# First four mixer outputs in four accumulator banks, statistics behind the third pack, value transposes one slot later, the fourth head's root behind the exponentials

## The chip, the core and the metric

The kernel runs on one core of a Trainium2 chip. A core has TensorE (PE, matrix products from SBUF into PSUM; PEld is its weight load), VectorE (DVE), ScalarE (ACT), GpSimd (POOL) and SyncE (SP), which here only issues the loads of the weights. The engines run their own instruction streams and meet only by semaphores. PSUM has eight banks of 128 x 512 fp32, called `ps[:, 0]` to `ps[:, 7]` here; bank 7 is `STAT`. The metric is the device time of one execution, in microseconds; lower is better.

## What is computed

Two transformer blocks on x of 512 tokens x 1024 features, all in fp32. The change touches only the first part of the first block, the hybrid mixer:

```python
def hybrid_mixer(h, w_in, lam_q1, ..., subln_g, w_out, rel_bias, layer_idx):
    proj = h @ w_in
    (aq, ak, av, bq, bk, bv, cq, ck, cv, iq, ik, iw) = jnp.split(
        proj, np.cumsum(IN_SPLITS)[:-1].tolist(), axis=-1)
    ...
    o_a = diff_attention(aq, ak, av, lam, lam_init, subln_g, rel_bias[:, :A_HEADS])
    o_b = dilated_attention(bq, bk, bv, rel_bias[:, A_HEADS:A_HEADS + B_HEADS])
    o_c = dsa_attention(cq, ck, cv, iq, ik, iw, rel_bias[:, A_HEADS + B_HEADS:])
    o = jnp.concatenate([o_a, o_b, o_c], axis=-1).astype(h.dtype)
    return o @ w_out

def first_block(x, mem, ...):
    h = rmsnorm(x, norm_mix[l])
    x = x + hybrid_mixer(h, ...)
    h = rmsnorm(x, norm_mem[l])
    x = x + memory_attention(h, rmsnorm(mem, norm_memkv[l]), ...)
    h = rmsnorm(x, norm_ffn[l])
    x = x + conv_ffn(h, ...)
```

`diff_attention` has four heads, each the difference of two softmaxes, and ends with an rmsnorm per head (`subln_g`). `dsa_attention` selects 128 keys per query by an indexer. The rest (memory attention, the convolutional feed-forward layer, and the second block with four feed-forward layers, a pool and long-convolution mixer and a latent attention) is outside the change.

## The kernel before

**Packs.** Every weight matrix is cut into packs of 128 outputs x 1024 inputs (512 KB). SP loads pack n into `raw[:, n % 2]`, ACT rounds it to `whi` (`split_high`), and a subtraction gives the rest, `wlo`; this is done by POOL (`split_low`, L693) for all packs but the first `FIRST` = 2, where DVE does it (`first_low`, L2000). SP loads pack n once pack n-2 is split. The input is split the same way, into `lin_hi` and `lin_lo`, 8 chunks of 128 x 512. A pack then takes 24 matmuls: for each chunk high x high (L741), high x low (L742), low x high (L743). So three passes give the precision of fp32.

**Start.** ACT and DVE make the eight chunks, and beside them the squares of x and their sum (`sumsq`). PE runs packs 0 and 1 chunk by chunk (L798 to L814), pack 1 two chunks behind pack 0, so that work starts before all of x is there. Before the last chunk of pack 1 it takes the column sum of `sumsq` (`stats(0)`, L755). ACT takes the root of it (L1360), DVE its reciprocal (L1904): `rstd`, by which every output of the mixer is scaled when DVE evicts it from PSUM (L2133). Then PE makes the bias rows (L818, L819), which DVE adds to a mask (L2027, L2028) before the reciprocal.

**Slots.** The 30 packs of the mixer run in slots n = 0 to 29, the outputs in order (`MIX_ORDER`): six indexer tiles, four heads of query, key and value of the differential attention, then the other heads. In slot n each engine does its pack work and then what `between(n)` asks: the indexer in slots 6 to 11, the scores of the differential attention from slot 10, `top_round`s of the key selection on DVE in slots 8 to 28, and so on. Pack n goes into bank n % 2, so its first matmul waits for the eviction of pack n-2. The engines' orders are written out by hand; the constants name the slots:

- Head h of the differential attention is multiplied out in slot 16 + 4h, its squares are summed by PE into bank 6 in slot 17 + 4h (`diff_sum`, L892), DVE reads the sum in slot 18 + 4h (L2119, into `diff_root[h]`), ACT takes the root in slot 19 + 4h (`diff_roots`, L1516: a logarithm and an exponential, with an activation table load before each), DVE scales the head in slot 20 + 4h (L2123).
- `turn_values(v, n)` (L841 to L851) transposes value tile v on PE into bank 6 too, in the slots `V_AT` = (12, 13, 15, 18, 22, 24, 27, 31); ACT copies it back (`store_values`). It must wait until DVE has read the sums made before.

**Pair steps.** After slot 29 come 18 steps s = 0 to 17 for the other eight heads, two at a time: PE scores (L939), DVE maximum (L2150), ACT exponentials (L1586), DVE division (`pair_norm`, L2160), PE transposes (`pair_turn`, L968), ACT copies (L1594), and every fourth step PE's product (L982). From s = 2 each step has one pack of the memory projection too (`memory_pack`, L954 to L956), whose one bank must be evicted (L2182) before the next. The step s also runs `between(30 + s)`. In step 3 ACT rounds all four heads of the differential attention to `o_hi` (L1610), in step 4 DVE makes their rests `o_lo` (L2172). Then `project_out` multiplies the eight chunks of `o_hi` and `o_lo` by `w_out`, each chunk of the first output waiting for the semaphore `mixed_low`.

## Time and profile before

| | us |
|---|---|
| median of 3 runs | 2858.08 |
| lowest, highest | 2857.74, 2867.32 |
| profiled execution, its time | 2862.86 |
| profiled execution, span of the trace | 2860.8 |
| PE busy | 2763.7 (97%) |
| PEld busy | 2180.9 (76%) |
| DVE busy | 1167.6 (41%) |
| POOL busy | 1123.0 (39%) |
| ACT busy | 1034.3 (36%) |
| mean DMA rate | 91 GB/s |

The views used are the page's chain of work that ended last, the timeline (one row for an instruction or a run of like instructions: start, duration of the whole run, engine, line, operation, tiles, count, and in brackets how long the engine had been idle and who released it), and tables of busy time by stretch. A matmul's duration overlaps with the next one's, so the distance of two starts is what it costs. PEclk is the clock granted to TensorE as a share of full speed: 1.00 is 2.4 GHz, 0.50 is 1.2 GHz.

### The profile page before, as it was taken

What the parts mean: (1) busy time and instruction counts of PE and PEld (TensorE: products, weight loads), DVE (VectorE), ACT (ScalarE), POOL (GpSimd) and SP (SyncE); (2) the same over time, 40 slices, a digit from 0 to 9 for tenths busy, and PEclk for the clock granted to TensorE, in tenths of its full rate; (3) what the DMA queues carried; (4) which work ended last, traced back from release to release, by engine and by line L of the source; (5) the groups of instructions that cost most, each with busy time, mean ns of one, the idle gap of its engine ahead of it and who ended that gap; (6) DMA issues with size and microseconds to landing.
All of it is one profiled execution on the core that took longest, in us unless ns stands there. A gap on an engine that the chain in (4) does not pass through costs nothing.

```text
span 2860.8 us, 35435 instructions
## 1 busy us (share of the span) xinstructions
PE 2763.7 (97%) x12322; PEld 2180.9 (76%) x12322; DVE 1167.6 (41%) x1919; ACT 1034.3 (36%) x1579; POOL 1123.0 (39%) x477
## 2 busy tenths in 40 slices
PE   7999999999999999999999999999999989999997
PEld 5766787888887888856878888888888744788886
DVE  4766534555535223138783222222221356322212
ACT  3445534444333232251223222233222557322222
POOL 2323442444454444522314444444444420444443
PEclk9999999999999999999999999999999999999998
DMA  4323331333332323321203333332333210233233
GB/s 148 113 82 103 111 96 45 97 95 96 100 107 87 97 94 97 116 81 64 73 23 103 95 95 97 109 103 90 101 95 108 84 52 1 81 95 98 93 103 103
DMA packets 77383, 259.70 MB, mean 91 GB/s; under 512 B 8871, under 2 KB 12455, under 8 KB 77048
## 3 DMA queue, kind: packets, MB, share of 16 engines
q1 hardware_dynamic: 68976, 242.77, 27.4%
q10 hardware_dynamic: 8328, 15.88, 1.7%
q8 instruction: 49, 0.80, 0.1%
q14 instruction: 30, 0.25, 0.0%
HBM read 252.59 MB, written 6.03 MB: 90 GB/s over the span
## 4 chain that ended last, share of the span: by engine, by line
PE 91%; DVE 5%; issue 2%; ACT 2%; DMA 0%; ACTq 0%; SPq 0%; DVEq 0%
PE ps L741 26%; PE ps L742 26%; PE ps L743 26%; PE ps L1274 1%; PE ps L1288 1%; PE ps L1302 1%; PE ps L1280 1%; PE ps L1089 1%; PE ps L1021 0%; PE ps L1031 0%; PE ps L954 0%; PE ps L1137 0%; PE ps L955 0%; PE ps L956 0%; PE ps L939 0%
## 5 line engine op out<-in xcount | busy, mean ns | idle before, releaser
L695 POOL TENSOR_TENSOR wlo<-raw,whi 128x1024 fp32r<-128x1024 f32 x453 | 1109.0, 2451 | 1699.1 <-ACT whi L1335 1698.3
L741 PE MATMUL ps<-lin_hi,whi 128*128 128x512 f32 x2208 | 871.4, 395 | 15.7 <-DVE waves_tmp L2296 6.6
L742 PE MATMUL ps<-lin_lo,whi 128*128 128x512 f32 x2208 | 863.5, 391 | 0.0
L743 PE MATMUL ps<-lin_hi,wlo 128*128 128x512 f32 x2208 | 863.2, 391 | 0.0
L1335 ACT ACTIVATE whi<-raw 128x1024 fp32r<-128x1024 f32 x455 | 476.7, 1053 | 524.1 <-PE ps L743 476.0
L741 PEld LDWEIGHTS ps<-lin_hi,whi 128*128 128x128 f32 x2208 | 417.3, 189 | 110.2 <-issue 15.3
L742 PEld LDWEIGHTS ps<-lin_lo,whi 128*128 128x128 f32 x2208 | 417.3, 189 | 88.2 <-issue 2.6
L743 PEld LDWEIGHTS ps<-lin_hi,wlo 128*128 128x128 f32 x2208 | 417.0, 189 | 88.0
L741 PE MATMUL ps<-act_hi,whi 128*128 128x512 f32 x880 | 342.6, 389 | 0.0
L743 PE MATMUL ps<-act_hi,wlo 128*128 128x512 f32 x880 | 342.4, 389 | 0.0
L742 PE MATMUL ps<-act_lo,whi 128*128 128x512 f32 x880 | 342.3, 389 | 0.0
L1917 DVE SCALAR_TENSOR_TENSOR x<-ps,x 128x512 f32 x72 | 49.8, 692 | 486.2 <-PE ps L743 486.2
L1950 DVE TENSOR_TENSOR up<-ps,rstd 128x512 f32<-128x512 f32 x88 | 60.8, 691 | 393.9 <-PE ps L743 393.9
L1426 ACT ACTIVATE act_hi<-hidden 128x512 f32 (+1 forms) x88 | 55.6, 632 | 458.8 <-DVE hidden L1973 458.8
L741 PEld LDWEIGHTS ps<-act_hi,whi 128*128 128x128 f32 x880 | 165.2, 188 | 35.4 <-POOL wlo L695 0.8
L743 PEld LDWEIGHTS ps<-act_hi,wlo 128*128 128x128 f32 x880 | 165.2, 188 | 34.6
L742 PEld LDWEIGHTS ps<-act_lo,whi 128*128 128x128 f32 x880 | 165.2, 188 | 34.5
L1350 ACT ACTIVATE scratch<-x 128x512 f32 x72 | 45.6, 634 | 262.0 <-DVE x L1917 262.0
L1950 DVE TENSOR_TENSOR gate<-ps,rstd 128x512 f32<-128x512 f32 x88 | 60.9, 692 | 188.2 <-PE ps L743 187.3
L741 PE MATMUL ps<-o_hi,whi 128*128 128x512 f32 x256 | 100.5, 392 | 1.7 <-DVE o_lo L2478 1.7
L742 PE MATMUL ps<-o_lo,whi 128*128 128x512 f32 x256 | 99.6, 389 | 0.0
L743 PE MATMUL ps<-o_hi,wlo 128*128 128x512 f32 x256 | 99.6, 389 | 0.0
(351 smaller groups left out, 2648.6 us busy)
## 6 DMA issues: line engine op xcount, KB each, us to landing
raw<-in_packs SPq DMA_DIRECT2D x459, 512.0 KB, 3.5
table<-bias_scratch ACTq DMA_DIRECT2D x12, 256.0 KB, 2.9
bias_scratch<-biasrow ACTq DMA_DIRECT2D x16, 160.0 KB
x<-in_x_t SPq DMA_DIRECT2D x4, 512.0 KB, 7.8
out_t<-x ACTq DMA_DIRECT2D x8, 256.0 KB, 2.2
bias_scratch<-biasrow ACTq DMA_DIRECT2D x4, 320.0 KB
mem<-in_mem_t ACTq DMA_DIRECT2D x1, 1024.0 KB, 7.7
pool_count<-in_pool_count ACTq DMA_DIRECT2D x1, 1024.0 KB, 4.8
```

Source lines behind the costliest of these rows:

```text
L695: pool.tensor_tensor(wlo[:, n % 4, :], raw[:, n % 2, :], whi[:, n % 4, :].bitcast(F32), ALU.subtract).then_inc(low_split, 1)
L741: pe.matmul(target, wh, hi[:, k, :], start=(k == 0), stop=False)
L742: pe.matmul(target, wh, lo[:, k, :], start=False, stop=False)
L743: mm = pe.matmul(target, wl, hi[:, k, :], start=False, stop=(k == total - 1))
L1089: pe.matmul(ps[:, 4 + c // 2, :], ones[:, :], filt_sq[t % 2][:, c * T:(c + 1) * T], start=(t == 0 and c % 2 == 0), stop=(t == QT - 1 and c ...
L1274: mm = pe.matmul(ps[:, 2 * p + h, :], q_nope[r:r + 64, 2 * g + p, cut], k_nope[r:r + 64, 2 * g + p, :], start=True, stop=False)
L1280: mm = pe.matmul(ps[:, j, :], q_rope[r:r + 32, g, cut], k_rope[r:r + 32, :], start=False, stop=True)
L1335: act.activation(whi[:, n % 4, :], raw[:, n % 2, :], ACT.Copy).then_inc(high_split, 1)
L1350: act.activation(squares[:, d % 2, :], x[:, row, :].rearrange("p a t -> p (a t)"), ACT.Square).then_inc(squares_ready, 1)
L1426: act.activation(act_hi[:, bass.ds(f, 1), :].rearrange("p a t -> p (a t)"), h_buf, ACT.Copy).then_inc(hidden_high, 1)
L1917: dve.scalar_tensor_tensor(out=xc, in0=ps[:, j, :], scalar=factor, in1=xc, op0=ALU.mult, op1=ALU.add).then_inc(outs_done, 1)
L1950: dve.tensor_tensor(target, ps[:, 2 * g + side, :], rstd[:, :], ALU.mult).then_inc(outs_done, 1)
```

## The change

It has three parts.

**Start.** Packs 0 to 3 get banks 0 to 3 (`mixer_bank`), so packs 2 and 3 wait for no eviction, packs 4 and 5 for those of packs 0 and 1. Pack 1 runs three chunks behind pack 0 (`LAG`). `stats(0)` and the bias rows come behind pack 2. DVE splits pack 2 as well (`FIRST_LOW` = 3); POOL begins with pack 3 and waits until the squares are summed. SP loads pack 1 before the third and fourth quarter of x. ACT does the chunks first and most squares afterwards; DVE sums all squares behind the chunks. The root on ACT is one slot later, and the bias addition on DVE moves from before the reciprocal to slot 1.

**Value transposes.** `V_AT` becomes (12, 13, 15, 19, 23, 24, 28, 32): tiles 3, 4, 6 and 7 one slot later.

**Fourth head.** Its root leaves step 1 for the end of step 16, behind the last exponentials and copies; its scale, rounding and rest are in step 17, and its buffer is `scratch[:, 0]`. Heads 0 to 2 are rounded in steps 0 to 2 (one each) and their rests made in steps 1 to 3, where before all four stood together in steps 3 and 4. The first output of `project_out` takes its chunks in the order 0, 1, 2, 4, 5, 6, 3, 7.

```diff
-FIRST = 2
+FIRST, FIRST_LOW = 2, 3
+LAG = 3
+def mixer_bank(n):
+    return n if n < 4 else n % 2
+MIXED_ORDER = (0, 1, 2, 4, 5, 6, 3, 7)
+LAST_HEAD = HEADS - 1
-V_AT = (12, 13, 15, 18, 22, 24, 27, STEPS_AT + 1)
+V_AT = (12, 13, 15, 19, 23, 24, 28, STEPS_AT + 2)
...
         load_x(0)
         load(0, None)
-        for q in range(1, 4):
+        load_x(1)
+        load(1, None)
+        for q in range(2, 4):
             load_x(q)
...
-        pool.wait_ge(low_split, FIRST)
-        for n in range(FIRST, 4):
+        pool.wait_ge(low_split, FIRST_LOW)
+        pool.wait_ge(squares_summed, DC)
+        for n in range(FIRST_LOW, 4):
             split_low(n, None)
...
         for n in range(FIRST, N_MIXER):
-            pe.wait_ge(outs_done, n - 1)
-            pack("mixer", None, 4, n, ps[:, n % 2, :], LIN)
+            if n >= 4:
+                pe.wait_ge(outs_done, n - 3 if n < 6 else n - 1)
+            pack("mixer", None, 4, n, ps[:, mixer_bank(n), :], LIN)
+            if n == 2:
+                pe.wait_ge(dve_order, 1)
+                stats(0)
+                bias_rows()
+                pe.wait_ge(ident_arrived, 16)
             between(n)
...
         for n in range(N_MIXER):
             split_high(AHEAD + n)
-            if n == 0:
+            if n == 1:
                 root(0)
...
-            if s == 3:
-                act.wait_ge(diff_scaled, HEADS)
-                for h in range(HEADS):
-                    act.activation(o_hi[:, h, :], diff_out[:, h, :], ACT.Copy).then_inc(out_high, 1)
             if s >= 5 and s % 4 == 1:
+                if s == LAST_STEP - 1:
+                    diff_high(LAST_HEAD)
...
+            if s < LAST_HEAD:
+                diff_high(s)
+            if s == PAIR_STEPS:
+                diff_roots(LAST_HEAD)
...
-            if s == 4:
-                for h in range(HEADS):
-                    dve.wait_ge(out_high, h + 1)
-                    dve.tensor_tensor(o_lo[:, h, :], diff_out[:, h, :], o_hi[:, h, :].bitcast(F32), ALU.subtract).then_inc(mixed_low, 1)
+            if s == LAST_STEP - 1:
+                diff_scale(LAST_HEAD)
+                diff_low(LAST_HEAD, 7)
...
+            if 1 <= s <= LAST_HEAD:
+                diff_low(s - 1, s)
```

Here `diff_high(h)` waits for the scaled head h and writes `o_hi[:, h]`, `diff_scale(h)` waits for its root and scales it, `diff_low(h, n)` waits for `out_high` = n and writes `o_lo[:, h]`.

**Where it moves instructions.** DVE at the start, from the first split of a pack to the first eviction; L2002 and L2031 are the split of a pack, L2010 and L2037 a chunk, L2018 and L2048 a sum of squares. Before:

```order
7 L2002 TENSOR_TENSOR wlo<-raw,whi 128x1024 [waits high_split,dve_order]
8 L2010 SCALAR_TENSOR_TENSOR lin_lo<-x,cols,lin_hi 128x512 [waits chunk_high,x_quarter0_arrived]
9 L2010 SCALAR_TENSOR_TENSOR lin_lo<-x,cols,lin_hi 128x512 [waits chunk_high]
10 L2018 TENSOR_TENSOR sumsq<-sumsq,scratch 128x512 [waits squares_ready]
11 L2010 SCALAR_TENSOR_TENSOR lin_lo<-x,cols,lin_hi 128x512 [waits chunk_high,x_quarter1_arrived]
12 L2018 TENSOR_TENSOR sumsq<-sumsq,scratch 128x512 [waits squares_summed,squares_ready]
13 L2010 SCALAR_TENSOR_TENSOR lin_lo<-x,cols,lin_hi 128x512 [waits chunk_high]
14 L2002 TENSOR_TENSOR wlo<-raw,whi 128x1024 [waits high_split]
```

After:

```order
7 L2037 SCALAR_TENSOR_TENSOR lin_lo<-x,cols,lin_hi 128x512 [waits chunk_high,x_quarter0_arrived,dve_order]
8 L2031 TENSOR_TENSOR wlo<-raw,whi 128x1024 [waits high_split]
9 L2037 SCALAR_TENSOR_TENSOR lin_lo<-x,cols,lin_hi 128x512 [waits chunk_high]
10 L2037 SCALAR_TENSOR_TENSOR lin_lo<-x,cols,lin_hi 128x512 [waits chunk_high,x_quarter1_arrived]
11 L2031 TENSOR_TENSOR wlo<-raw,whi 128x1024 [waits high_split]
...
17 L2031 TENSOR_TENSOR wlo<-raw,whi 128x1024 [waits high_split]
18 L2048 TENSOR_TENSOR sumsq<-sumsq,scratch 128x512 [waits squares_ready]
19 L2048 TENSOR_TENSOR sumsq<-sumsq,scratch 128x512 [waits squares_summed,squares_ready] x7
```

The sums no longer stand between the chunks; all eight follow the third split.

PE in slots 17 to 19, the packs' own matmuls left out; L862 and L876 are scores, L873 and L887 transposes of probabilities, L892 and L906 the sum of squares of head 0, L850 and L864 the transpose of value tile 3. Before:

```order
502 L892 MATMUL ps<-scratch,ones 128x512 [waits v_stored,diff_squares]
...
531 L873 MATMUL ps<-ident,probs 128x128 [waits mixer_copied,mixer_ready]
532 L873 MATMUL ps<-ident,probs 128x128 x2
533 L850 MATMUL ps<-ident,proj 128x128 [waits diff_sums_read,v_stored,outs_done]
534 L850 MATMUL ps<-ident,proj 128x128 x3
...
561 L873 MATMUL ps<-ident,probs 128x128 [waits mixer_copied,mixer_ready]
```

After:

```order
502 L906 MATMUL ps<-scratch,ones 128x512 [waits v_stored,diff_squares]
...
531 L887 MATMUL ps<-ident,probs 128x128 [waits mixer_copied,mixer_ready]
532 L887 MATMUL ps<-ident,probs 128x128 x2
...
559 L887 MATMUL ps<-ident,probs 128x128 [waits mixer_copied,mixer_ready]
560 L887 MATMUL ps<-ident,probs 128x128 x3
561 L864 MATMUL ps<-ident,proj 128x128 [waits diff_sums_read,v_stored,outs_done]
```

The value transpose stands one whole pack and its scores later; what it waits for stays the same.

ACT in steps 0 to 3; L1586 and L1609 are the exponentials, L1594 and L1617 the copies of transposed probabilities, L1518 and L1519 the fourth head's root, L1523 and L1546 the copy of a value tile. Before:

```order
164 L1586 ACTIVATE pair_probs,small<-pair_probs,small 128x256 x2
165 L1335 ACTIVATE whi<-raw 128x1024
166 L1518 ACT_TABLE_LOAD
167 L1518 ACTIVATE diff_late<-diff_late 128x512
168 L1519 ACT_TABLE_LOAD
169 L1519 ACTIVATE diff_late<-diff_late 128x512
170 L1523 ACTIVATE proj<-ps 128x512
171 L1594 ACTIVATE pair_probs_t<-ps 128x128 x2
172 L1586 ACTIVATE pair_probs,small<-pair_probs,small 128x384 x2
...
178 L1610 ACTIVATE o_hi<-proj 128x512 x4
```

After:

```order
158 L1622 ACTIVATE o_hi<-proj 128x512
159 L1609 ACTIVATE pair_probs,small<-pair_probs,small 128x256 x2
160 L1355 ACTIVATE whi<-raw 128x1024
161 L1617 ACTIVATE pair_probs_t<-ps 128x128 x2
162 L1622 ACTIVATE o_hi<-proj 128x512
163 L1609 ACTIVATE pair_probs,small<-pair_probs,small 128x384 x2
164 L1355 ACTIVATE whi<-raw 128x1024
165 L1546 ACTIVATE proj<-ps 128x512
...
167 L1622 ACTIVATE o_hi<-proj 128x512
```

The two table loads and two activations of the root are gone from between the exponentials; the roundings stand singly.

## Rows read from the trace of the kernel before

**Rows 1.** The page's chain of work that ended last, shares by engine.
```profile
PE 91%; DVE 5%; issue 2%; ACT 2%; DMA 0%; ACTq 0%; SPq 0%; DVEq 0%
```

**Rows 2.** Timeline of PE at the start: start, duration, line, count, idle before.
```profile
10.75 0.76 PE L808 MATMUL ps<-lin_hi,whi 128*128 128x512 f32 x1 [10.75 <-DVE lin_lo L2010]
...
17.22 0.51 PE L808 MATMUL ps<-lin_hi,whi 128*128 128x512 f32 x1 [2.29 <-DVE wlo L2002]
...
28.11 1.10 PE L755 MATMUL ps<-sumsq,ones 128*128 128x512 f32 x2 [0.79 <-DVE relb_apart L2019]
...
30.76 0.38 PE L819 MATMUL ps<-onehot,relb_apart 32*96 32x128 f32 x2
...
36.93 0.76 PE L741 MATMUL ps<-lin_hi,whi 128*128 128x512 f32 x1 [5.79 <-issue]
...
45.04 0.39 PE L741 MATMUL ps<-lin_hi,whi 128*128 128x512 f32 x1
...
50.48 0.39 PE L741 MATMUL ps<-lin_hi,whi 128*128 128x512 f32 x1
```

**Rows 3.** Timeline of the other engines at the start.
```profile
8.72 1.23 DVE L2002 TENSOR_TENSOR wlo<-raw,whi 128x1024 fp32r<-128x1024 f32 x1 [2.65 <-ACT whi L1335]
...
21.39 5.23 POOL L695 TENSOR_TENSOR wlo<-raw,whi 128x1024 fp32r<-128x1024 f32 x2 [20.94 <-ACT whi L1335]
...
24.29 3.67 DVE L2018 TENSOR_TENSOR sumsq<-sumsq,scratch 128x512 f32<-128x512 f32 x2
...
29.24 0.69 ACT L1360 ACTIVATE rstd<-ps,small 128x512 f32<-128x512 f32 x1 [5.75 <-PE ps L755]
...
32.11 3.34 DVE L1904 RECIPROCAL rstd<-rstd 128x512 f32<-128x512 f32 x1
...
36.14 1.29 DVE L2133 TENSOR_TENSOR proj<-ps,rstd 128x512 f32<-128x512 f32 x2
```

**Rows 4.** Busy time by stretch: length, PE, PEld, DVE, ACT, POOL, then PEclk, DMA.
```profile
10.70:28.60 17.90, 14.77 (x46) 10.95 (x47) 15.55 (x22) 10.70 (x16) 5.23 (x2) 0.90 0.43 141
36.90:50.40 13.50, 13.47 (x48) 10.93 (x49) 1.22 (x2) 2.55 (x3) 2.40 (x1) 0.80 0.27 82
162.60:171.50 8.90, 8.80 (x28) 6.94 (x28) 3.73 (x10) 7.60 (x12) 2.38 (x1) 0.66 0.24 78
198.90:206.50 7.60, 7.58 (x28) 5.95 (x28) 2.67 (x6) 6.14 (x10) 2.39 (x1) 0.78 0.12 27
260.80:267.00 6.20, 6.20 (x33) 4.37 (x34) 2.67 (x9) 4.37 (x12) 2.37 (x1) 0.72 0.27 73
120.00:140.00 20.00, 20.00 (x99) 16.01 (x98) 19.34 (x51) 12.38 (x30) 7.18 (x3) 1.00 0.37 114
```

**Rows 5.** Timeline of PE in slots 18 and 22: the value transposes.
```profile
162.69 1.08 PE L850 MATMUL ps<-ident,proj 128*128 128x128 f32 x4 [2.51 <-DVE diff_early L2119]
...
198.92 0.66 PE L850 MATMUL ps<-ident,proj 128*128 128x128 f32 x4 [3.14 <-DVE diff_early L2119]
```

**Rows 6.** Timeline of the pair steps, several engines.
```profile
255.62 1.28 ACT L1518 ACT_TABLE_LOAD   x1
...
259.52 0.75 DVE L2123 SCALAR_TENSOR_TENSOR proj<-proj,small,diff_late 128x512 f32<-128x512 f32 x1 [3.19 <-ACT diff_late L1519]
...
260.80 1.12 PE L968 MATMUL ps<-ident,pair_probs 128*128 128x128 f32 x4 [2.59 <-DVE pair_probs L2160]
...
270.47 4.63 DVE L2172 TENSOR_TENSOR o_lo<-proj,o_hi 128x512 fp32r<-128x512 f32 x4
...
272.04 2.52 POOL L695 TENSOR_TENSOR wlo<-raw,whi 128x1024 fp32r<-128x1024 f32 x1 [2.17 <-ACT whi L1335]
...
275.58 0.36 PE L954 MATMUL ps<-mem_hi,whi 128*128 128x256 f32 x1 [2.77 <-DVE mem_k L2182]
...
337.06 1.08 ACT L1594 ACTIVATE pair_probs_t<-ps 128x512 f32<-128x512 f32 x2 [1.43 <-PE ps L968]
...
342.57 0.50 PE L741 MATMUL ps<-o_hi,whi 128*128 128x512 f32 x1
```

124 lines of the change are left out of this document (67 added, 57 removed).

## The prediction

> **What bounds the kernel now.** I read the chain of work that ended last first: TensorE holds 91% of it [rows 1], so only what lets PE start earlier, closes an idle stretch of PE or raises its clock can move the time. Then the waits of PE over the mixer, from the start to 345 us, and behind each the timeline, to see who was late. They are few. Work starts at 10.75 us, then PE waits 2.29, 0.79 and 5.79 us [rows 2]; 2.51 and 3.14 us in slots 18 and 22 [rows 5]; 2.59 and 2.77 us in the pair steps [rows 6]. A wait costs more than its length: the table by stretch shows what PE was granted after it. After the 5.79 us it ran at 0.80 for 13.5 us, after 2.51 at 0.66 for 8.9 us, after 3.14 at 0.78 for 7.6 us, after 2.59 at 0.72 for 6.2 us, while the undisturbed stretch from 120 to 140 has 1.00 [rows 4]. The lost time is (1 - PEclk) x length: 2.7, 3.0, 1.7 and 1.7 us. After the 2.77 us I see no such fall, so a wait may cost its length alone. The levels are 1.2 and 2.4 GHz.
>
> **Start, removed.** Before, pack 4 starts at 50.48 [rows 2]. For the changed kernel I lay out PE's work anew. A pack at full clock is the distance of packs 3 and 4, 50.48 - 45.04 = 5.44 us [rows 2].
> - First matmul: the first split of a pack by DVE ended at 8.72 + 1.23 = 9.95 [rows 3], and PE then waited for the second thing, a chunk, until 10.75. Now that chunk is made ahead of the split: 10.0.
> - Packs 0 to 2 without a break: 3 x 5.44 = 16.3 us.
> - Low clock at the beginning: 0.10 x 17.9 = 1.8 us were lost in the first stretch, 2.7 us in pack 2 [rows 4]. I take 2.5, between them and nearer the upper one, since this stretch too follows a long rest.
> - Statistics and bias rows: 28.11 to 30.76 + 0.38 = 31.14, less the three matmuls (0.7) between them: 2.3 us [rows 2].
> - Pack 3: 5.4 us.
>
> Sum: 10.0 + 16.3 + 2.5 + 2.3 + 5.4 = 36.5 for the start of pack 4, **14.0 us earlier**.
>
> It holds only if nobody is late. *Chunks:* pack 1 follows three chunks behind, so its split is wanted when PE has done three chunks, at 10.0 + 3 x 1.28 (low clock) = 13.8. Before, it came at about 17.2 [rows 2], because ACT waited for pack 1's load, the last of six; now it is the fourth, some 3 us earlier, and DVE should be done at 13.3. *DVE's split of pack 2:* after the last chunk (about 16.7), so about 18.6; wanted near 23.4. *Sums:* eight of about 0.8 us behind it, to about 25.3; wanted at 28.8. Before, two sums took 3.67 us and stood beside two splits of POOL, 21.39 to 26.6 [rows 3]; now POOL waits for them, and I take them unhindered. *POOL:* its two splits took 5.23 us [rows 3], so 2.6 each: pack 3 is split at about 28, wanted at 31.1; pack 4 at about 30.5, wanted at 36.5. *Evictions:* here the change adds the waits for the evictions of packs 0 and 1 ahead of packs 4 and 5. Statistics start at 28.8; root 1.13 later (29.24 - 28.11), 0.69 long; reciprocal 3.34; from its end to the first eviction 0.69, the eviction about 0.65 [rows 3]: 35.4. PE wants the bank at 36.5. This is the nearest margin, 1.1 us, and since both sides hang on the same statistics, it doesn't move with the clock much. The bias addition (two operations of the first's kind, 1 us) now stands behind the second eviction, not ahead of the reciprocal. Queued behind it are ACT's copies of the bias rows to DRAM and ACT's next split, wanted only by pack 6 at 47. SP's queue gets one load ahead of two others, which costs the late quarters of x under 3 us; they are wanted from about 13.
>
> **Value transposes.** In slot 18 PE waits until DVE has read the sum of squares, which DVE does near the end of its slot, behind an eviction that itself waits for pack 18. One slot later the read is 6 us old. The wait goes with the clock's fall: slot 18 gives 2.51 + 3.0 = 5.5 us, slot 22 gives 3.14 + 1.7 = 4.8 us [rows 4, 5]; the transposes themselves (0.66 us at mostly full clock [rows 5]) only move. What is late next? In slots 19 and 23 ACT has the root, four operations of about 3.9 us, ahead of the copy that PE's next transposes need; it can start once the sum is read and ends about 3 us before the copy could start anyway. **10.3 us**, bounds 8 and 10.5.
>
> **Pair steps.** The root in step 1 ran on ACT from 255.62 and DVE's scale came to wait 3.19 us for it, until 259.52; `pair_norm` stood behind the scale, and PE waited 2.59 us [rows 6]. With the root gone DVE can do the division about 2 us earlier. I count 1.8 of the 2.59 us, plus the clock's 1.7 us [rows 4]. The transposes of the last value tile leave step 1, where PE waits for the first division anyway, and stand in step 2, where nobody waits: 0.66 us lost [rows 5]. The 2.77 us wait was for an eviction that stood behind four rests of 4.63 us in all [rows 6]; they are spread over three steps now, and each follows the eviction. I count 2.5. Sum: 1.8 + 1.7 - 0.7 + 2.5 = 5.3; I take **5.0**, bounds 2 and 6.5.
>
> At this place a rule of the chip speaks against the change. The row: the four rests, two-input operations from SBUF, took 4.63 us where an eviction from PSUM of the same size takes 0.65 (1.29 for two [rows 3]), and a split of POOL ran from 272.04 to 274.56 among them [rows 6]; the last one ended just behind it. So a rest that meets a split can cost its length plus up to 2.5 us. The Trainium skill (SBUF — State Buffer, "SBUF: two separate sides") states why: a VectorE instruction with two SBUF inputs and a GpSimd instruction exclude one another for the whole instruction, and whoever starts first keeps the ports; so the trace agrees. By the rule four rests in a row meet one split and pay once, three rests in three steps can pay three times.
>
> **Fourth head at the end.** Its root now starts behind the last copies, 337.06 + 1.08 = 338.1, and ends at about 342.0; scale, rounding and rest follow by 344.3, the last chunk's rest by 345.4. PE starts the output projection at 342.57 [rows 6] and takes 0.68 us a chunk; with the fourth head seventh and the last product eighth it wants them at 346.7 and 347.3. Cost 0; without the new order it would wait some 2 us at the fourth chunk. ACT's splits of two later packs come 2 us later; they are wanted 5 us and more later.
>
> **Sum.** 14.0 + 10.3 + 5.0 + 0 = 29.3 us. The profiled execution took 2862.86 us, which gives 2833.6; it lies 4.8 above the median of the runs, and from the median 2858.08 I get **2828.8**. Nothing after the mixer changes, and PE bounds it there.
>
> **Rivals.**
> - *The sums stay slow.* At 3.67 / 2 = 1.84 us each [rows 3] they end at 18.6 + 14.7 = 33.3, POOL's split of pack 3 at 35.9, and pack 3 starts 4.8 us late, with 2.7 us of clock behind it. Start part 6.5, time 2836. For it: the rows' own price; against: POOL was at work then. Chance 0.10.
> - *The rests meet the splits.* Each of three rests is held up to 2.5 us and the next scores with it; if two reach PE, 5 us are lost and the first fall of the clock stays, 1.7. Pair part -2, time 2836. For it the row above; against, DVE had 2 to 3 us to spare in most steps. Chance 0.12.
> - *The change doesn't do what it says* in slots 19 and 23: ACT's root, copy and value copy in one slot are late for PE's next transposes, and the wait comes back one slot on. 2 to 3 of the 10.3 us remain, time 2836. Chance 0.06.
> - *Slower than before.* DVE, not PE, bounds the slots. DVE is busy 19.34 of 20 us from 120 to 140 [rows 4], and the two waits I remove are also its time to catch up. If the new phase of POOL's splits holds up a DVE operation in each slot by 2.4 us, PE waits for it and loses about as much again by the clock: 4.8 us a slot. From six slots on that eats the whole gain; in fourteen (12 to 25) it is 67 us, time 2896. Against it: PE is busy 20.00 in that same stretch, and DVE idles 5 us in slots 18 and 22 after the reads. Chance 0.03.
>
> **How the numbers follow.** Forecast 0.69. Its own range is 2826 to 2836 (start 12 to 15, slots 8 to 10.5, pair steps 2 to 6.5). The first three rivals lie at 2836, two of them together near 2843; so 2822 to 2842 holds 8 in 10, with the scatter of the runs (2857.74 to 2867.32). Half a percent, about what a measurement of this kernel can tell from no change, is 14.3 us: below 2843.8. That takes the start alone. Faster 0.90, within 0.5% 0.07 (two or three rivals at once), slower 0.03.
>
> **What would show it.** Pack 4's first matmul near 36.5, no wait of PE over 1 us between 14 and 160; no wait at the value transposes and PEclk 1.00 through slots 18 to 24; in the pair steps no wait over 1.5 us for DVE in steps 2 and 5; no wait for `o_lo` at the output projection. Wrong would be: a wait for POOL's `wlo` ahead of pack 3, for DVE's evictions ahead of pack 4, for chunks between 13 and 17, or rests of over 2 us in steps 1 to 3 with PE waiting behind them.

## The result and the profile after

The changed kernel takes **2833.12 us** (median of 4 runs, 2833.00 to 2835.70) against 2859.18 for the kernel before, measured beside it (4 runs, 2857.74 to 2867.32). The ratio is 0.9904, with a 95% interval of 0.9891 to 0.9916: about 27 us faster. The forecast was 2828.8 with a range of 2822 to 2842.

| | before | after |
|---|---|---|
| median, us | 2859.18 | 2833.12 |
| profiled execution: time, us | 2862.86 | 2835.70 |
| its span, us | 2860.8 | 2833.5 |
| waits of PE up to 345 us, without that for its first matmul | 24.3 | 5.0 |

First the waits of PE from the start to 345 us, after: engine, tile and line, what it waited for; us in total, times, longest.

```profile
PE ps L823 <- DVE wlo L2031: 10.2, 1, 10.2
PE ps L988 <- DVE pair_probs L2198: 4.6, 4, 2.0
PE ps L876 <- DVE small L2108: 0.4, 1, 0.4
```

Before there were nine such lines. The two of the start (2.29 and 5.79 us), both value transposes and the wait for `mem_k` in step 5 are gone; what is left, 4.6 us, waits for the division of the pair steps. Now the timeline of PE at the start, after. The rows answer to [rows 2]: the columns are start, duration, line, what it does, its count, and in brackets the idle time before it.

```profile
10.23 0.77 PE L823 MATMUL ps<-lin_hi,whi 128*128 128x512 f32 x1 [10.23 <-DVE wlo L2031]
...
28.83 1.02 PE L770 MATMUL ps<-sumsq,ones 128*128 128x512 f32 x2
...
30.72 0.38 PE L834 MATMUL ps<-onehot,relb_apart 32*96 32x128 f32 x2
31.02 0.50 PE L756 MATMUL ps<-lin_hi,whi 128*128 128x512 f32 x1
...
36.59 0.39 PE L756 MATMUL ps<-lin_hi,whi 128*128 128x512 f32 x1
```

Pack 4 starts at 36.59 instead of 50.48, and no bracket stands between 10.23 and 36.59. The first matmuls run at low clock all the same: until 14.64 they start 0.43 us apart, from 14.96 on 0.23. The column PEclk doesn't show this; two stretches, eleven matmuls in the first and 24 in the second:

```profile
10.23:14.90 4.67, 4.67 (x11) 3.72 (x12) 4.32 (x7) 4.57 (x8) 0.00 (x0) 1.00 0.99 358
15.00:20.00 5.00, 5.00 (x24) 4.10 (x23) 4.26 (x6) 3.47 (x6) 0.00 (x0) 1.00 0.32 98
```

The other engines there, answering to [rows 3]:

```profile
8.86 1.23 DVE L2031 TENSOR_TENSOR wlo<-raw,whi 128x1024 fp32r<-128x1024 f32 x1
...
16.83 1.23 DVE L2031 TENSOR_TENSOR wlo<-raw,whi 128x1024 fp32r<-128x1024 f32 x1 [0.53 <-ACT whi L1355]
17.97 6.26 DVE L2048 TENSOR_TENSOR sumsq<-sumsq,scratch 128x512 f32<-128x512 f32 x8
...
30.61 3.35 DVE L1933 RECIPROCAL rstd<-rstd 128x512 f32<-128x512 f32 x1 [5.81 <-ACT rstd L1380]
34.66 1.29 DVE L2171 TENSOR_TENSOR proj<-ps,rstd 128x512 f32<-128x512 f32 x2
```

```profile
24.37 5.03 POOL L709 TENSOR_TENSOR wlo<-raw,whi 128x1024 fp32r<-128x1024 f32 x2 [23.92 <-DVE sumsq L2048]
```

Eight sums take 6.26 us: each is 0.68 to 0.70 long, and they start 0.8 apart. Before, two took 3.67 beside POOL [rows 3], one of them 2.88. POOL starts when the sums are done. The busy time by stretch answers to [rows 4], in its columns; the first two stretches are the start and pack 4's, the next two follow the places of the old waits in slots 18 and 22, the last two begin with the first matmul after the two longest waits that are left:

```profile
10.70:28.60 17.90, 17.90 (x71) 14.54 (x71) 12.46 (x23) 12.34 (x17) 4.23 (x2) 1.00 0.41 138
36.60:50.10 13.50, 13.50 (x61) 11.20 (x60) 3.92 (x8) 4.56 (x5) 4.99 (x3) 1.00 0.46 155
148.70:157.60 8.90, 8.90 (x45) 7.02 (x44) 8.18 (x25) 8.78 (x12) 2.38 (x1) 1.00 0.25 79
179.50:187.10 7.60, 7.60 (x40) 5.95 (x39) 7.29 (x21) 7.54 (x14) 2.38 (x1) 1.00 0.30 78
229.40:239.40 10.00, 9.99 (x60) 7.81 (x61) 8.18 (x18) 8.34 (x21) 7.76 (x3) 0.83 0.34 106
287.10:297.10 10.00, 9.99 (x59) 7.09 (x60) 3.40 (x12) 3.68 (x9) 2.37 (x1) 0.83 0.32 97
```

In the third and fourth stretch PE is busy without a gap and PEclk is 1.00, where [rows 4] have 0.66 and 0.78. The pair steps, answering to [rows 6]:

```profile
229.41 0.53 PE L988 MATMUL ps<-ident,pair_probs 128*128 128x128 f32 x2 [1.97 <-DVE pair_probs L2198]
...
229.87 2.45 DVE L2130 TENSOR_TENSOR o_lo<-proj,o_hi 128x512 fp32r<-128x512 f32 x1 [0.32 <-ACT o_hi L1622]
...
287.11 0.66 PE L988 MATMUL ps<-ident,pair_probs 128*128 128x128 f32 x4 [1.74 <-DVE pair_probs L2198]
...
314.45 0.50 PE L756 MATMUL ps<-o_hi,whi 128*128 128x512 f32 x1
```

**Where the 27 us come from.** The same instruction is looked for in both timelines, and the differences of its starts are the gain so far:

| PE's instruction | before | after | gain so far | of this part |
|---|---|---|---|---|
| first matmul | 10.75 | 10.23 | 0.52 | 0.52 |
| pack 4 | 50.48 | 36.59 | 13.89 | 13.37 |
| scores of slot 20 | 178.24 | 158.83 | 19.41 | 5.5 |
| first pair scores | 250.86 | 226.51 | 24.35 | 4.9 |
| product of step 5 | 278.62 | 248.99 | 29.63 | 5.3 |
| output projection | 342.57 | 314.45 | 28.12 | -1.5 |
| end of the span | 2860.8 | 2833.5 | 27.3 | -0.8 |

Each of the two columns of starts is one profile. The last two rows give something back: the experiments show why for the first of them; the second lies within what profiles differ by behind the mixer (below).

### The profile page after: what moved, and what is told of

The parts are those of the page before. It is cut to its first block, busy times and chain, and to the rows that moved or that the text cites. A ratio compares the mean times of both kernels' runs of the same rounds, so it can differ in the third digit from the quotient of the medians.

```text
span 2833.5 us, 35433 instructions
## 1 busy us (share of the span) xinstructions
PE 2753.8 (97%) x12322; PEld 2176.3 (77%) x12322; DVE 1172.4 (41%) x1920; ACT 1034.5 (37%) x1579; POOL 1121.2 (40%) x476
## 4 chain that ended last, share of the span: by engine, by line
PE 92%; DVE 5%; ACT 1%; issue 1%; DMA 0%; ACTq 0%; DVEq 0%
PE ps L756 26%; PE ps L758 26%; PE ps L757 26%; PE ps L1294 1%; PE ps L1308 1%; PE ps L1322 1%; PE ps L1300 1%; PE ps L1109 1%; PE ps L974 1%; PE ps L1041 0%; PE ps L1051 0%; PE ps L975 0%; PE ps L976 0%; PE ps L959 0%; PE ps L876 0%
## 5 line engine op out<-in xcount | busy, mean ns | idle before, releaser
L756 PEld LDWEIGHTS ps<-act_hi,whi 128*128 128x128 f32 x880 | 165.2, 188 | 35.9 <-POOL wlo L709 0.8
```

What stands on the lines that cost most here:

```text
L756: pe.matmul(target, wh, hi[:, k, :], start=(chunk0 + at == 0), stop=False)
```

## Experiments

In each run the time is compared with the kernel before on the same chip. For differences of one or two us the starts of PE's instructions say more than the times, and this is why: from the output projection to the end all kernels run the same instructions, yet the profiles need 2513.5 to 2519.2 us for them.

**The parts alone.** Three kernels are the kernel before with one part of the change each.

*Start alone*, the kernel before with all of the change's first part; its core:

```diff
-FIRST = 2
+FIRST, FIRST_LOW = 2, 3
+LAG = 3
...
+def mixer_bank(n):
+    return n if n < 4 else n % 2
...
-        for q in range(1, 4):
+        load_x(1)
+        load(1, None)
+        for q in range(2, 4):
```

> The kernel before with the start part alone (four banks, statistics behind pack 2, loads, splits and squares in the new order). My theory, that the parts add up because PE alone bounds the mixer: pack 4 starts at 36.6 and everything behind it comes 13.9 us earlier, the waits at the value transposes (2.51 and 3.14 us) and in the pair steps stay as they were. Time 13.9 us under the kernel before, ratio 0.9951. Rival, that another engine takes part of it back (DVE bound in slots 10 to 28): pack 4 at 36.6, but the scores of slot 18 less than 13 us earlier, total gain under 10 us.

*Values alone*, the kernel before with

```diff
-V_AT = (12, 13, 15, 18, 22, 24, 27, STEPS_AT + 1)
+V_AT = (12, 13, 15, 19, 23, 24, 28, STEPS_AT + 2)
```

> The kernel before with the value transposes alone moved one slot. My theory, a wait costs its length plus a fall of the clock: no wait of PE in slots 18 and 22, PEclk 1.00 through slots 18 to 24, gain 5.5 + 4.9 = 10.4 us by the first scores of the pair steps, of which the last transpose (now in step 2) gives back up to 0.7. Ratio 0.9965. Rival, that only the waits count and the clock's fall comes from elsewhere: PEclk still falls in these slots and the gain is 5.7 us, ratio 0.998. Rival, ACT's root is late in slots 19 and 23: a new wait of PE for the copies there, gain under 5 us.

*Fourth head alone*, the kernel before with the third part of the change:

```diff
+MIXED_ORDER = (0, 1, 2, 4, 5, 6, 3, 7)
+LAST_HEAD = HEADS - 1
...
+            if s < LAST_HEAD:
+                diff_high(s)
+            if s == PAIR_STEPS:
+                diff_roots(LAST_HEAD)
```

> The kernel before with the fourth head's part alone: its root behind the exponentials, roundings and rests of heads 0 to 2 one a step, chunk order of the output projection. The last value tile is still turned in step 1. My theory: the waits of 2.59 us (step 2) and 2.77 us (step 5) and the clock's fall behind the first go, 2.59 + 1.7 + 2.77 = up to 7 us by the product of step 5; since PE's transposes of the value tile fill part of the wait of step 1, there is no fall of the clock there. Ratio 0.9976 to 0.998. Rival, the three rests each meet a split of POOL and reach PE: gain 0 to 3 us by step 5.

| | median, us | ratio to before (95%) | output projection at | earlier by |
|---|---|---|---|---|
| before | 2861.61 | | 342.57 | |
| start alone | 2849.95 | 0.9957 (0.9943 to 0.9971) | 329.62 | 12.95 |
| values alone | 2850.85 | 0.9963 (0.9949 to 0.9978) | 332.53 | 10.04 |
| fourth head alone | 2853.95 | 0.9975 (0.9964 to 0.9987) | 335.73 | 6.84 |
| all | 2833.12 | 0.9904 (0.9891 to 0.9916) | 314.45 | 28.12 |

The parts add up: 12.95 + 10.04 + 6.84 = 29.8 us of starts against 28.1 for all, and 0.43 + 0.37 + 0.25 = 1.05% of time against 0.96%, with each interval some 0.13% to either side. All three are needed for the result, the start and the values most. In start alone both waits at the value transposes stay (2.51 and 3.14 us); in values alone PE has no wait over 0.4 us between 100 and 242 us; in fourth head alone the waits of 2.59 and 2.77 us are gone. A part of the fourth head's 6.84 isn't its own: the first turn of the pair steps already stood at 251.47 instead of 253.76, 2.29 us earlier, ahead of anything that it changes there. Without it the parts make 27.5. Values alone loses again what it had ahead: its first turn of the pair steps stands 11.4 us earlier than before (242.38), but its wait of 2.95 us in step 5 is followed by the largest fall of all, 0.69 over 10 us, where the kernel before had none behind 2.77 us.

**The clock after a wait.** This kernel is the one before, with 13 matmuls of no use in slot 22, where PE waited 3.14 us; they write to a bank that nobody reads at that time.

```diff
+            if n == 22:
+                pe.wait_ge(mem_sums_read, 1)
+                for k in range(13):
+                    pe.matmul(ps[:, STAT, :], lin_hi[:, k % 8, 0:P], lin_hi[:, k % 8, :], start=True, stop=True)
```

> The kernel before with 13 extra matmuls of 512 columns in slot 22, ahead of the value transpose, into a bank that nobody uses then and that nobody reads: they add work that the result doesn't need and lie in the wait of 3.14 us. My theory, that the clock falls because PE stood idle: the wait shrinks to some 0.2 us, PEclk stays 1.00 behind it and pack 23 takes 5.4 instead of 7.2 us, so that the scores of slot 23 come 1.7 us earlier though PE does more. Slot 18 is as before. Total gain 1.7 us, ratio 0.9994, which the times can hardly tell; the trace decides. Rival, that the fall has another cause (time, power, the slots' load): PEclk about 0.78 from 199 to 206.5 as before, total no change or up to 1 us slower.

Measured: 2859.08 us (2856.59 to 2862.58), ratio 0.9992 (0.9982 to 1.0002), no difference that the times can show; the output projection stands at 340.67, 1.90 us earlier. The timeline of PE, and the two stretches of 10 us behind slot 22's and slot 18's transposes:

```profile
192.73 3.22 PE L917 MATMUL ps<-lin_hi 128*128 128x512 f32 x13
196.10 0.63 PE L850 MATMUL ps<-ident,proj 128*128 128x128 f32 x4 [0.16 <-DVE diff_early L2123]
```

```profile
196.10:206.10 10.00, 10.00 (x49) 7.92 (x50) 6.30 (x19) 8.26 (x16) 2.40 (x1) 1.00 0.22 57
162.70:172.70 10.00, 10.00 (x49) 7.92 (x50) 7.30 (x23) 9.22 (x14) 2.40 (x1) 1.00 0.20 70
```

Behind the filled wait PEclk is 1.00, as a cause in the idle time would have it (the kernel before has 0.83 there). But the second row spoils it as a proof: slot 18's wait of 2.52 us, untouched, has no fall behind it either, where the kernel before had the largest:

```profile
162.70:172.70 10.00, 10.00 (x37) 7.74 (x38) 4.59 (x14) 8.78 (x13) 2.38 (x1) 0.70 0.21 69
```

So the price of a wait is not fixed, and the filler alone doesn't show that idle time is the cause. All profiles of this study together, 14 with those of the two kernels, have 36 waits of 1.7 to 3.2 us between 100 and 345 us; I took PEclk over the 10 us behind each, as in the rows above, and (1 - PEclk) x 10 as lost:

| wait | how many | with a fall | lost by one, mean | most |
|---|---|---|---|---|
| 2.2 to 3.2 us | 16 | 12 | 1.5 us | 3.1 |
| 1.7 to 2.0 us | 20 | 10 | 0.8 us | 1.7 |
| 0.94 to 0.98 us, with no longer one in the next 10 us | 6 | 0 | 0 | 0 |

The wait of 1.73 us in step 13 is the cleanest case, since it is there in twelve of these profiles at the same place of the program, with the same work behind it: five have 0.83 behind it and seven 1.00. What decides between them these runs don't settle; it isn't the length of the wait.

The (1 - PEclk) x 10 is also not what a fall costs in time. Between two fixed instructions the distances are alike to 0.2 us but for the falls:

| profile | first pair scores to product of step 5 | product of step 5 to output projection |
|---|---|---|
| changed kernel, two profiles | 22.48, 22.47 (fall in step 1) | 65.46, 65.42 (fall in step 13) |
| POOL early (below) | 22.33 (fall) | 63.95 (none) |
| bias addition first (below) | 21.75 (none) | 63.95 (none) |

The fall in step 13, 1.7 by the clock, costs 1.5 us; the one in step 1, 1.7 as well, only 0.6 to 0.7. Without it PE comes earlier to step 2 and waits there 0.56 us for a division.

At the start there is a second sign that chance has a part. In nine profiles with the new start (the changed kernel twice, start alone, and six of the kernels below) the first matmul stands at 9.98 to 10.23, but the first one faster than 0.63 us comes between 13.3 and 15.8, and the statistics stand at 28.17 to 29.38. The Trainium skill (TensorE: Matmul & The Clock Gate, "What's actually happening") says that the window in which the chip looks at the engine runs free and doesn't start with the kernel, so that the moment of a switch depends on where in it the work lands. The spread at the start agrees with that; no run here shows the window itself, and none shows that it decides about the falls behind the waits.

**The last two waits.** Four kernels on one chip: the changed kernel once more, two edits to it, and both edits together.

The changed kernel again, as the yardstick:

> The changed kernel itself, once more, as the yardstick for the three kernels beside it. In its first profile 1.97 us of waiting in pair step 1 and 1.74 us in step 13 were each followed by a stretch of low clock (1.6 and 1.7 us lost), while the same waits had no fall behind them in some of the other profiles. Theory A (the fall belongs to the wait and to the place): a new profile of the same kernel shows both falls again, the product of step 5 starts at 249.0 and the output projection at 314.5 within 0.2. Theory B (whether a wait of 2 us is followed by a fall changes between executions): the times of the runs spread over 2 to 4 us, in steps, and the profile may show one fall, both or none, with the output projection at up to 3.3 us earlier than 314.45. Time by both: about 0.990 of the kernel before.

Its profile shows both falls again, 0.83 behind each wait, the product of step 5 at 248.94 and the output projection at 314.36, as its theory A says of a profile. The five runs lie in two groups, 2832.6 and 2832.8 and 2834.9 to 2835.6, as its theory B says of the times; only one of the upper group has a profile. So two profiles of the same kernel agree, and whether the lower group had fewer falls stays open.

The last value tile goes back to step 1, ahead of the turn of the pair probabilities:

```diff
-V_AT = (12, 13, 15, 19, 23, 24, 28, STEPS_AT + 2)
+V_AT = (12, 13, 15, 19, 23, 24, 28, STEPS_AT + 1)
```

> The changed kernel with the last turn of values put back into pair step 1, where it stood before, ahead of the turn of the pair probabilities. In the changed kernel TensorE waits there 1.97 us for the division, and before it waited 0.98 and 0.36 with the turn between. Theory A: the turn moves into the wait, 0.63 us of the following slot are saved, and the low clock after 1.97 us (0.84 in 232 to 236 in the first profile, 1.6 us lost in all) is gone too, since no wait is over 1 us: 0.6 to 2.3 us faster than the changed kernel. Theory B (the clock falls whatever the length): 0.6 us faster, no more. If the turn came from elsewhere late (its eviction is then the wait of 0.98), nothing is gained.

ACT rounds the weights behind its two copies in steps 4, 8 and 12, so POOL's split of them comes later:

```diff
-            if s < PAIR_STEPS + KV_FROM:
+            if s < PAIR_STEPS + KV_FROM and s not in (4, 8, 12):
                 split_high(N_MIXER + AHEAD + s)
...
                 pair_copy(2 * s - 2)
                 pair_copy(2 * s - 1)
+            if s in (4, 8, 12):
+                split_high(N_MIXER + AHEAD + s)
```

> The changed kernel with ScalarE's rounding of the weights in pair steps 4, 8 and 12 put behind the two copies of the transposed probabilities, so that GpSimd's split of those weights begins some 2 us later and does not stand beside VectorE's two divisions of 512 elements. Those took 4.41 us beside a split of GpSimd (4.92 us for two) where a pair of 384 took 0.75. Theory A (the wait of 1.74 us in step 13 comes from the lock of the two engines): the divisions fall to about 1 us, the wait of 1.74 is gone, with the low clock behind it where there was one; 1.7 to 3.4 us faster than the changed kernel. Theory B (the divisions are late for another reason, the roots and sums ahead of them): the wait stays at 1.7, no difference. If GpSimd's split then meets another operation of VectorE, or the weights come late for their pack, a new wait of 1 to 2.5 us stands in steps 5, 9 and 13, and it is slower.

Both:

> The two edits together: last turn of values in step 1, ScalarE's rounding behind the copies in steps 4, 8 and 12. If both work and are independent, the sum: 2.3 to 5.7 us faster than the changed kernel, no wait of TensorE over 1 us left in the mixer. If the length alone counts: 2.3 us. If the lock is not the cause of step 13's wait: 0.6 to 2.3 us.

| | median of runs, us (range) | ratio to before (95%) | PE's output projection at |
|---|---|---|---|
| changed kernel | 2834.90 (2832.62 to 2835.56) | 0.9906 (0.9892 to 0.9919) | 314.36 |
| last turn back | 2833.43 (2833.06 to 2834.51) | 0.9905 (0.9890 to 0.9920) | 312.75 |
| rounding late | 2832.46 (2827.83 to 2833.23) | 0.9899 (0.9885 to 0.9912) | 311.97 |
| both | 2829.75 (2827.62 to 2832.07) | 0.9889 (0.9874 to 0.9904) | 311.83 |

Last turn back, PE in step 1 and 2, and the stretch behind step 13's wait:

```profile
228.97 0.63 PE L864 MATMUL ps<-ident,proj 128*128 128x128 f32 x4 [0.98 <-DVE scratch L2160]
229.96 0.53 PE L988 MATMUL ps<-ident,pair_probs 128*128 128x128 f32 x2 [0.36 <-DVE pair_probs L2198]
235.35 0.70 PE L988 MATMUL ps<-ident,pair_probs 128*128 128x128 f32 x4 [0.95 <-DVE pair_probs L2198]
```

```profile
286.90:296.90 10.00, 9.99 (x72) 7.40 (x73) 4.84 (x16) 4.40 (x11) 2.35 (x1) 1.00 0.31 107
```

The wait of 1.97 is 0.98 + 0.36 again, and neither has a fall behind it. But step 2 now waits 0.95 where the changed kernel didn't. The product of step 5 comes 21.75 us behind the first pair scores, against 22.47 in the changed kernel with its fall and 21.75 in the profile of the table above that had none. So the edit gains nothing where the clock doesn't fall, and 0.7 us where it does. (By plain starts this is hidden: 248.81 against 248.94, since this profile was 0.58 late by the statistics already.) The other 1.5 us at the output projection come from step 13, whose wait of 1.73 this time had no fall behind it; that is not the edit's doing.

Rounding late does remove a wait. DVE in step 12 of the changed kernel and of the kernel with both edits, with POOL at the same time:

```profile
282.64 4.41 DVE L2198 TENSOR_SCALAR pair_probs<-pair_probs,small 128x512 f32<-128x512 f32 x2
...
281.85 4.92 POOL L709 TENSOR_TENSOR wlo<-raw,whi 128x1024 fp32r<-128x1024 f32 x2 [2.89 <-ACT whi L1355]
```

```profile
282.91 2.29 DVE L2200 TENSOR_SCALAR pair_probs<-pair_probs,small 128x512 f32<-128x512 f32 x2
...
288.65 3.99 DVE L2200 TENSOR_SCALAR pair_probs<-pair_probs,small 128x128 f32<-128x128 f32 x2
```

```profile
282.12 2.40 POOL L709 TENSOR_TENSOR wlo<-raw,whi 128x1024 fp32r<-128x1024 f32 x1 [2.89 <-ACT whi L1355]
...
287.79 4.77 POOL L709 TENSOR_TENSOR wlo<-raw,whi 128x1024 fp32r<-128x1024 f32 x2 [3.27 <-ACT whi L1355]
```

With one split of POOL beside them instead of two, the divisions of 512 take 2.29 instead of 4.41 us, and PE's wait of 1.74 is gone. The second split now meets the divisions of 128 that follow: 3.99 us instead of 0.48. They are early enough that PE waits only 0.36 for the second of them:

```profile
292.69 0.33 PE L988 MATMUL ps<-ident,pair_probs 128*128 128x128 f32 x1 [0.36 <-DVE pair_probs L2200]
```

So the cause is shown (a division of DVE stands still while POOL splits), and the edit moves the meeting to a place with more room. But its worth is small. Such a wait is new behind the products of step 5, 9 and 13 each (0.30, 0.36 and 0.37 us in rounding late), and from the product of step 5 to the output projection this kernel needs 63.69 us, against 63.95 with the old wait and no fall and 65.42 with the fall: 0.25 us gained where no fall comes, and 1.5 more where the clock would have fallen.

Both edits together have the lowest median of this study, 5.1 us below the changed kernel's, and no run of one lies among the runs of the other, though only 0.55 us lie between. The mixer accounts for half of it: the output projection stands 2.5 us earlier (0.1 at the first pair scores, 0.7 by the product of step 5, 1.7 behind it). Where the rest comes from isn't shown.

**Single steps of the start and of the rests.** Four more kernels on another chip, each the changed one with one thing taken back. The changed kernel itself didn't run beside them, so their times are set against the kernel before and against each other.

The loads in their old order:

```diff
         load_x(0)
         load(0, None)
-        load_x(1)
-        load(1, None)
-        for q in range(2, 4):
+        for q in range(1, 4):
             load_x(q)
+        load(1, None)
```

> The changed kernel with the second pack's weights loaded behind all four quarters of x again, as before the change; all else as changed. In the changed kernel TensorE begins at 10.2 and never waits in its first packs. Theory A (the order of the loads is what removed the wait of 2.29 us): it is back, 2 to 3 us, between 14 and 17 us, with more low clock behind it, and the third pack of the mixer, 31.02 in the changed kernel, starts 2 to 4.5 us later. Theory B (the chunks come sooner by the order of VectorE's and ScalarE's instructions, whatever the loads): no wait over 1 us, the third pack within 0.5 of 31.02. Time by A: 0.9915 of the kernel before instead of 0.9905, by B the same.

Measured: 2836.92 us (2833.73 to 2839.83), ratio 0.9921 (0.9898 to 0.9944).

```profile
16.63 0.80 PE L822 MATMUL ps<-lin_hi,whi 128*128 128x512 f32 x1 [2.42 <-DVE lin_lo L2036]
17.22 0.63 PE L823 MATMUL ps<-lin_lo,whi 128*128 128x512 f32 x1
```

The old wait is back, 2.42 us, in front of the fourth chunk, and pack 3 starts at 35.66 instead of 31.02. That is 4.6 us, a little above what I had given: nearly as much again as the wait is lost to low clock, since a matmul behind it takes 0.63 us until 21.1, where in the changed kernel it takes 0.39 from 14.96 on. This exchange of two loads alone is a third of the start's gain. At the output projection (316.86) only 2.4 of the 4.6 us are left: neither the wait of step 1 nor that of step 13 has a fall behind it in this profile, which by the table above is worth 0.7 and 1.5.

The bias addition ahead of the reciprocal:

```diff
+        dve.wait_ge(bias_ready, 1)
+        order(dve.tensor_tensor(biasrow[:, 0:512], ps[0:12 * APART, 4, :], maskrow[:, 0:512], ALU.add))
...
         norm(0)
...
-            if n == 1:
-                dve.wait_ge(bias_ready, 1)
```

> The changed kernel with the addition of the bias rows back ahead of the reciprocal on VectorE. It takes 0.67 and about 0.3 us, waits for the bias matmuls that end near 31.1, and pushes the reciprocal from 30.6 to about 32 and the two first evictions from 34.66 and 35.3 to about 36.0 and 36.7. Pack 4 started at 36.59 in the changed kernel with no wait. Theory A (the evictions hold pack 4, as the prediction's nearest margin of 1.1 us says): pack 4 waits 0.3 to 0.5, pack 5 not, less than 1 us in all. Theory B (the bank is not what it would wait for): no wait. Time by both within 0.1% of the changed kernel; what tells is the start of pack 4 and of the reciprocal.

```profile
31.52 3.34 DVE L1933 RECIPROCAL rstd<-rstd 128x512 f32<-128x512 f32 x1
...
35.55 2.48 DVE L2169 TENSOR_TENSOR proj<-ps,rstd 128x512 f32<-128x512 f32 x4
```

```profile
35.37 0.39 PE L756 MATMUL ps<-lin_hi,whi 128*128 128x512 f32 x1
...
36.29 0.50 PE L756 MATMUL ps<-lin_hi,whi 128*128 128x512 f32 x1
```

Pack 4 follows 0.92 us behind the last chunk of pack 3 instead of 0.67 (36.59 - 35.92 in the changed kernel): it waits 0.25 us for the first eviction, which ends near 36.2. So the margin ahead of pack 4 was there, and moving the bias addition away was worth a quarter of a microsecond. The time, 2830.97 us (ratio 0.9901, 0.9878 to 0.9925), can't show that: two runs lie at 2827.6 and 2827.9 and two at 2834.1 and 2834.2, though all four execute the same instructions. In its profile, taken from the first pair, the waits of 1.98 and 1.72 us in the pair steps stand as always and neither has a fall behind it.

Roundings and rests of three heads in one block each:

```diff
+            if s == 3:
+                for h in range(LAST_HEAD):
+                    diff_high(h)
...
+            if s == 4:
+                for h in range(LAST_HEAD):
+                    diff_low(h, h + 1)
...
-            if 1 <= s <= LAST_HEAD:
-                diff_low(s - 1, s)
```

> The changed kernel with the mixer's heads 0 to 2 rounded together in pair step 3 and their rests together in step 4, as before the change, in place of one head a step. Theory A (the block of rests on VectorE held the product of step 5, and GpSimd beside it made it longer: 4.63 us for four before, 2.45 for one beside GpSimd and 0.68 for one alone): three rests take 2 to 3.7 us, and TensorE waits 1 to 2.8 us in front of the products of step 5, which started at 245.9 in the changed kernel, 248.99 for the product that waited before. Some 1 to 3 us slower by step 5, partly given back since the rest that met GpSimd's splits in step 1 (1.97 us of waiting there for the division) is gone: that wait should then stay, because it follows the square root and the division ahead of the rest, not the rest. Theory B (the rests never were on the path; step 5 waited for something else): no wait in step 5, and the time unchanged.

```profile
243.06 4.04 DVE L2131 TENSOR_TENSOR o_lo<-proj,o_hi 128x512 fp32r<-128x512 f32 x3
...
247.58 0.36 PE L974 MATMUL ps<-mem_hi,whi 128*128 128x256 f32 x1 [2.35 <-DVE mem_k L2223]
```

```profile
244.10 2.44 POOL L709 TENSOR_TENSOR wlo<-raw,whi 128x1024 fp32r<-128x1024 f32 x1 [1.64 <-ACT whi L1355]
```

The wait in step 5 is back, 2.35 us. The product of step 5 comes 24.75 us behind the first pair scores, 2.3 more than in the changed kernel. Three rests take 4.04 us, of which 3 x 0.68 = 2.0 are their own and 2.0 the meeting with POOL's split of 2.44. The time is 2834.70 us (2833.58 to 2837.32), ratio 0.9914 (0.9893 to 0.9935), against 0.9901 and 0.9903 for the kernels with the bias addition and POOL's split moved, on the same chip: some 3 to 4 us, though the intervals overlap. The wait of 1.98 in step 1 stays, though no rest stands there any more. So it has nothing to do with the rest that met POOL in step 1.

POOL splits pack 2 and doesn't wait for the sums:

```diff
-FIRST, FIRST_LOW = 2, 3
+FIRST, FIRST_LOW = 2, 2
...
-        pool.wait_ge(squares_summed, DC)
...
-        first_low(2)
```

> The changed kernel with the rests of pack 2 computed by GpSimd as before, without its wait for the sums of squares, so that GpSimd's splits stand beside VectorE's eight sums. In the changed kernel eight sums took 6.26 us from 17.97 (0.78 each), in the kernel before two took 3.67 us beside GpSimd. Theory A (the two engines lock each other): GpSimd's splits start near 15 to 18, some of the sums take 2 to 2.5 us instead of 0.78, and the sums end 2 to 5 us later than 24.2 though VectorE has one split less to do (1.23); the statistics at 28.83 have a margin of 4 us, so pack 4 starts at 36.6 or up to 1.5 us later. Theory B (no lock, the sums of before were slow because they waited for ScalarE's squares): sums 0.78 each, ending at 23. Time by A 0 to 1.5 us more than the changed kernel, by B the same.

```profile
16.84 2.39 POOL L709 TENSOR_TENSOR wlo<-raw,whi 128x1024 fp32r<-128x1024 f32 x1 [16.40 <-ACT whi L1354]
23.07 5.74 POOL L709 TENSOR_TENSOR wlo<-raw,whi 128x1024 fp32r<-128x1024 f32 x2 [3.83 <-ACT whi L1354]
```

```profile
16.13 10.43 DVE L2046 TENSOR_TENSOR sumsq<-sumsq,scratch 128x512 f32<-128x512 f32 x8
...
26.70 2.13 DVE L2049 TENSOR_SCALAR relb_apart<-relb 32x12 f32<-32x12 f32 x1
```

The sums take 10.43 us instead of 6.26. Line 2046 by itself, with the shortest, the middle and the longest of the eight in ns:

```profile
L2046 DVE TENSOR_TENSOR sumsq<-sumsq,scratch x8: 684/692/2867, 16.1 to 23.9; 128x512 f32<-128x512 f32 x8
```

Two of the eight, one beside each of POOL's first two splits, take up to 2.87 us, the others 0.68 to 0.70. The third split meets an operation on 32 x 12 elements, 0.17 us in the changed kernel and 2.13 here. The sums' 4.2 us stay on DVE and don't reach PE: the statistics start at 28.17 and pack 3 2.20 behind them, against 2.19 in the changed kernel. Time 2831.38 us (2827.69 to 2834.72), ratio 0.9903 (0.9881 to 0.9925). The order that keeps POOL out of the sums is right by its mechanism and worth nothing at this place.

## Why the prediction held, and where its steps were off

- **The sum**: 29.3 us foreseen, 27.3 by the spans and 26.1 by the medians. What lies behind the mixer differs by up to 5.8 us between profiles, so no more can be read from the ends. The 2828.8 is 4.3 below the time measured: 3.2 for the sum, and 1.1 because the kernel before itself had 2859.18 this time.
- **Start**, 14.0 foreseen for pack 4, 13.89 measured. The terms agree one by one: first matmul 10.0, measured 10.23; packs 0 to 2 with low clock 16.3 + 2.5 = 18.8, measured 28.83 - 10.23 = 18.60; statistics and bias 2.3, measured 31.02 - 28.83 = 2.19; pack 3 5.4, measured 5.57. The 2.5 us for low clock agree (18.60 less 16.3 is 2.3), but the rows that I took them from don't show this term: PEclk reads 1.00 over the nine slow matmuls at the start of the kernel before, as it does over the eleven here, and the 0.10 x 17.9 belongs to a fall behind its wait of 2.29 us. So the size is in part luck, and it varies: in the nine profiles with the new start pack 4 stands between 35.9 and 37.1. DVE's third split ended at 18.1 (foreseen 18.6), its sums at 24.2 (25.3), POOL's split of pack 3 stood near 26.9 (28). The rival of slow sums is out, and the last experiment says more: even where they were slow, PE didn't wait. I had priced that rival at 4.8 us with sums of 1.84 us each, taken from two sums beside two splits. A split holds DVE up once, not every sum: of the eight beside POOL two were long.
- **Nearest margin**: the first eviction done at 35.4, bank wanted at 36.5. Measured 34.66 + 0.65 = 35.3 and 36.59. The bias addition, put back, used these 1.3 us up and 0.25 more.
- **Value transposes**, 10.3 foreseen (5.5 and 4.8), 5.5 + 4.9 measured. The waits are gone and don't come back a slot later, PE is busy 8.90 of 8.90 and 7.60 of 7.60 us. That it came out to the tenth is in part luck: the two falls of the clock that I counted with 3.0 and 1.7 us were those of one profile. In start alone, fourth head alone and the filler kernel, the same wait of slot 18 lost 1.5, 1.7 and 0 us. What can be counted on is 2.5 + 3.1 us of length and a mean share for the clock.
- **Pair steps**, 5.0 foreseen. By the product of step 5 the gain is 5.3, as the sum of the terms said (5.3). The terms were right in kind (no wait for the root, no wait behind four rests), but two things stood beside them. I wrote that PE waits for the first division in step 1 anyway, and didn't price it: taking the value transposes out joined the two waits of 0.98 and 0.36 into one of 1.97, which in five of eight profiles had a fall of 1.7 us behind it, 0.7 of them felt at the product of step 5. The second is step 13.
- **What failed**: "After the 2.77 us I see no such fall, so a wait may cost its length alone" was the right doubt, applied to one term only. The wait of 1.73 us in step 13, in both kernels, had no fall behind it before and one of 1.7 us in the profile after. This is the -1.5 us between step 5 and the output projection: 65.46 us where seven profiles without the fall need 63.9 to 64.3. I had no term for it, since the change touches nothing there. That a change which moves the whole program draws the falls of all its waits anew is my reading; the runs show only that the falls differ from kernel to kernel.
- **The rests against POOL's splits**: the rule of the ports from the Trainium skill (SBUF — State Buffer, "SBUF: two separate sides") agrees with the trace: the first rest began behind a split, at 229.87 against 229.40, and took 2.45 us. The other two began 0.28 and 0.12 us ahead of one and took 0.68 each, and there the split took 2.66 and 2.82 us instead of 2.4. That they came first, by so little, is luck; the prediction had not worked out the order. The same rule names VectorE's two-port modes beside the operations with two inputs, and I had left the divisions out, which have one input: beside POOL they made the wait of step 13. Whether they run in such a mode no view shows, only that they are held up. The one rest that met a split held nothing up on PE, and the block of three put the wait of 2.35 back. Between pay once in a place where PE waits behind it, and pay once where nobody does, the second is better.
- **Fourth head at the end**, 0 foreseen and 0 measured: no wait for `o_lo`. But it was nearer than I wrote. DVE's last two rests, and PE's first matmuls of the seventh and eighth chunk:

```profile
315.43 2.48 DVE L2130 TENSOR_TENSOR o_lo<-proj,o_hi 128x512 fp32r<-128x512 f32 x1 [0.72 <-ACT o_hi L1622]
...
318.17 0.68 DVE L2213 TENSOR_TENSOR o_lo<-ps,o_hi 128x512 fp32r<-128x512 f32 x1
```

```profile
318.71 0.39 PE L756 MATMUL ps<-o_hi,whi 128*128 128x512 f32 x1
...
319.39 0.39 PE L756 MATMUL ps<-o_hi,whi 128*128 128x512 f32 x1
```

The fourth head's rest met a split (2.48 us) and ended 0.8 us ahead of its chunk, the last product's 0.5 ahead of its own. I had 2.4 and 1.9 there, and it wasn't in my list of margins.

## What to carry to other kernels

Lay out the new timeline of the engine that bounds, term by term from the durations of the rows: where the change only removes waits and the other engines' margins are worked out too, it comes close: within 0.2 us over 26 here, though low clock at the start alone moves that place by 1.2 us between profiles. Count a wait of 2 us or more as its length plus a share for the clock, not as the fall that one profile shows behind it, and check by the distance of two fixed instructions what a fall costs in time; and judge differences of a few us by the start of the same instruction in both timelines, since the whole time can differ by 6 us between runs of the same kernel.

When two engines can't run beside one another, look for who waits behind the one that is held up, not for how often they meet.
